# Expert stage of a decoder step: rows gathered by quarters and turned in 32x32 blocks by VectorE, gate/up weights loaded with 8 rows a partition

## The reference

```
a = jnp.einsum('td,edf->tef', t, w_gate)
b = jnp.einsum('td,edf->tef', t, w_up)
hid = (jax.nn.silu(a) * b * gates[:, :, None].astype(a.dtype)).astype(t.dtype)
out = jnp.einsum('tef,efd->td', hid, w_down)
...
x = x + g2[:, None, :] * hier_moe(h2, ...)
```

## Time and profile before

| | us |
|---|---|
| median of 3 runs | 1177.94 |
| lowest, highest | 1176.96, 1178.39 |
| span of the profiled execution (first to last instruction) | 1181.0 |
| TensorE busy | 1083.1 (92%) |
| VectorE busy | 777.0 (66%) |
| ScalarE busy | 508.2 (43%) |
| GpSimd busy | 295.5 (25%) |

### The profile page before, as it was taken

How to read it: one execution, slowest core, us unless ns; L and a number is a source line. 1 busy time by engine, 2 the same in 40 slices (tenths; PEclk the granted TensorE clock), 3 DMA queues, 4 the chain that set the end, 5 groups by cost and what they waited for, 6 DMA issues and landing times. The chain is left out here.

```text
span 1181.0 us, 18306 instructions
## 1 busy us (share of the span) xinstructions
PE 1083.1 (92%) x5541; PEld 804.7 (68%) x5542; DVE 777.0 (66%) x1276; ACT 508.2 (43%) x715; POOL 295.5 (25%) x359
## 2 busy tenths in 40 slices
PE   4799999999958899999999989999999999999992
PEld 2357777676646667777787646787878777778760
DVE  5456575756879973369887778555666555555385
ACT  5133242421132325436665344555555444444373
POOL 0046262616041000030000002333333323333344
PEclk9799999999989999999999989999999999999996
DMA  9834646557677459485766456897789777775597
GB/s 285 304 107 119 194 138 180 147 155 218 195 212 143 145 157 234 175 232 204 250 221 223 162 214 236 238 289 220 214 255 281 214 213 216 214 212 108 111 356 304
DMA packets 169247, 244.77 MB, mean 207 GB/s; under 512 B 66240, under 2 KB 124384, under 8 KB 167088
## 3 DMA queue, kind: packets, MB, share of 16 engines
q1 hardware_dynamic: 140833, 171.06, 45.8%
q0 software_dynamic: 16112, 54.88, 18.3%
q10 hardware_dynamic: 12246, 18.14, 4.6%
HBM read 169.36 MB, written 75.84 MB: 208 GB/s over the span
## 5 line engine op out<-in xcount | busy, mean ns | idle before, releaser
L126 PE MATMUL experts_psGU<-weights_we_hi,experts_x_hi 128*128 (+1 forms) x344 | 143.3, 417 | 2.7 <-issue 1.5
L128 PE MATMUL experts_psGU<-weights_we_lo,experts_x_hi 128*128 (+1 forms) x344 | 136.0, 395 | 0.0
L127 PE MATMUL experts_psGU<-weights_we_hi,experts_x_lo 128*128 (+1 forms) x344 | 135.9, 395 | 0.0
L126 PE MATMUL front_psM<-front_hT_hi,front_w_hi 128*128 128x512 f32 x256 | 107.0, 418 | 0.8 <-DVE front_hT_lo L1008 0.8
L128 PE MATMUL front_psM<-front_hT_lo,front_w_hi 128*128 128x512 f32 x256 | 101.5, 397 | 0.0
L127 PE MATMUL front_psM<-front_hT_hi,front_w_lo 128*128 128x512 f32 x256 | 101.5, 396 | 0.0
L2496 POOL DMA_INDIRECT acc_d<-experts_o_sb,experts_to_col x40 | 68.4, 1711 | 130.8 <-issue 64.8
L126 PEld LDWEIGHTS experts_psGU<-weights_we_hi,experts_x_hi 128*128 128x128 f32 x344 | 64.6, 188 | 28.5 <-issue 15.5
L2670 DVE TENSOR_TENSOR experts_x_lo<-experts_psX,experts_x_hi 128x1024 fp32r<-128x1024 f32 x42 | 51.4, 1225 | 37.5 <-ACT experts_x_hi L2560 37.5
L2660 DVE TENSOR_TENSOR weights_we_lo<-weights_we_raw,weights_we_hi (+1 forms) x64 | 75.5, 1221 | 0.0
L128 PEld LDWEIGHTS experts_psGU<-weights_we_lo,experts_x_hi 128*128 128x128 f32 x344 | 64.6, 188 | 15.5
(11 more groups left out here) (521 smaller groups left out, 2534.0 us busy)
## 6 DMA issues: line engine op xcount, KB each, us to landing
front_raw<-in_w_ada SPq DMA_DIRECT2D x32, 512.0 KB, 4.1
weights_we_raw<-in_exp_w_gate SPq DMA_DIRECT2D x16, 1024.0 KB, 6.0
weights_we_raw<-in_exp_w_up SPq DMA_DIRECT2D x16, 1024.0 KB, 12.5
weights_wd_raw<-in_exp_w_down SPq DMA_DIRECT2D x16, 1024.0 KB, 13.2
front_xraw<-in_x_prompt SPq DMA_DIRECT2D x4, 2048.0 KB, 10.7
front_raw<-in_w_ada SPq DMA_DIRECT2D x8, 1024.0 KB, 14.3
part_d<-middle_ev ACTq DMA_DIRECT2D x16, 512.0 KB, 3.0
middle_xt<-in_x_prompt SPq DMA_DIRECT2D x16, 512.0 KB, 4.7
```

Of the source, the lines that this page charges most:

```text
L126: pe.matmul(out, l_hi, r_hi, start=start, stop=False)
L127: pe.matmul(out, l_lo, r_hi, start=False, stop=False)
L128: return pe.matmul(out, l_hi, r_lo, start=False, stop=stop)
```

## The change

Three things change, and what follows from them:

1. The gate/up weights are read with 8 rows a partition, `(p k) f` instead of `(k p) f`, so that a partition's share of a matrix is one run of 8 KB in DRAM instead of 8 runs of 1 KB. `we_raw` holds gate and up apart. Index k of the contraction now stands for rows 8p + k, so the gathered rows must be turned to the same order.
2. A tile is gathered by four indirect DMAs instead of one, each with 128 pieces of 1 KB, a quarter of a row. Piece c brings, for tokens 32c to 32c+31, quarter q to the 32 partitions of quadrant q. The table of quarter indices `R.quart` is made once in `routing`: four small matmuls with `pick`, and a few steps on VectorE.
3. VectorE turns the tile with one transpose in 32x32 blocks from `xg` to `x_t`, which lies over `x_lo`. TensorE keeps only the turns of tiles 0 and 1. `x_hi` is cast from `x_t`, and `x_lo` is `x_t - x_hi` in place, both inputs in SBUF. The turn is now made two tiles ahead (`turn(s + 2)`) where it was one. The splits move: the down half and `PART1` now stand ahead of silu on ScalarE and ahead of hid on VectorE (`before`), `PART2` stays at the end (`behind`). The down half of an expert is split one tile later than before, and so its buffer is loaded later.

```
     def gather(self, pool, R, h2_d, t, u):
-        pool.tensor_copy(self.ic[:, u, :], R.idx[:, bass.ds(t, 1)]).then_inc(self.ic_ok, 1)
+        quarters = h2_d.rearrange("t (q n) -> (t q) n", q=4)
+        pool.tensor_copy(self.ic[:, u, :], R.quart[:, bass.ds(4 * t, 4)]).then_inc(self.ic_ok, 1)
         pool.wait_ge(self.ic_ok, t + 1)
         pool.sem_inc(self.fence, 1)
-        pool.indirect_dma_start(self.xg[:, u, :], None, h2_d, bass.IndirectOffsetOnAxis(self.ic[:, u, :], 0)
-                                ).then_inc(self.xg_in[u], 16)
+        for c in range(4):
+            pool.indirect_dma_start(self.xg[:, u, c * D // 4:(c + 1) * D // 4], None, quarters,
+                                    bass.IndirectOffsetOnAxis(self.ic[:, u, c:c + 1], 0)).then_inc(self.xg_in[u], 16)
...
-            sp.dma_start(self.wraw[:, u, :, i * FH:(i + 1) * FH], a[n][0, e].rearrange("(k p) f -> p k f", p=P)
-                         ).then_inc(self.raw_in[u], 16)
+            sp.dma_start(self.wraw[:, u, i], a[n][0, e].rearrange("(p k) f -> p k f", p=P)).then_inc(self.raw_in[u], 16)
...
+            def turn(t, u):
+
+                dve.wait_ge(xg_in[u], 32 * t + 16 - 32 * u)
+                dve.wait_ge(gu_mm, t - 1)
+                dve.transpose(xt[:, u].rearrange("p k (c i) -> p c k i", c=4),
+                              xg[:, u, :].rearrange("p (c j k) -> p c k j", c=4, k=KD)).then_inc(xt_ok, 1)
...
             with dve.Fori(1, end + 1, 2) as t:
                 for d in range(2):
                     u = 1 - d
                     s = t + d
-                    code = code_of(dve, s)
                     hidden_lo(s - 1)
+                    before(s)
                     hidden(s, u)
-                    x_lo_of(s + 1, 1 - u)
+                    turn(s + 2, u)
                     out(s - 1, 1 - u)
-                    with dve.If((code & 1) > 0):
-                        after = dve.snap((code >> 2) + 1)
-                        split_gu(after, PART2)
-                        split_d(after)
-                    with dve.If((code & 2) > 0):
-                        split_gu(dve.snap((code >> 2) + 2), PART1)
+                    x_lo_of(s + 2, u)
+                    behind(s)
...
@@ expert_pe
                     gate_up(s, u, now)
-                    turn(s + 1, 1 - u)
                     down(s - 1, before)
```

The new helpers on VectorE (ScalarE's are the same, with its casts):

```
+            def down_half(s):
+                code = code_of(dve, s - 1)
+                with dve.If((code & 1) > 0):
+                    split_d(dve.snap((code >> 2) + 1))
+                return code
+
+            def before(s):
+                code = down_half(s)
+                with dve.If((code & 2) > 0):
+                    split_gu(dve.snap((code >> 2) + 2), PART1)
+
+            def behind(s):
+                code = code_of(dve, s)
+                with dve.If((code & 1) > 0):
+                    split_gu(dve.snap((code >> 2) + 1), PART2)
```

154 lines of the change are left out of this document (91 added, 63 removed).

## The result

| | us |
|---|---|
| kernel before, median of 4 runs beside it | 1178.16 |
| changed kernel, median of 4 runs (lowest, highest) | 1204.71 (1203.77, 1207.84) |
| ratio | 1.0216, 95% interval 1.0199 to 1.0233 |
| predicted | 1173, range 1154 to 1192 |

The change makes the kernel 26.5 us slower. The page of the profile after has these lines: the span, busy time, TensorE's clock in 40 slices, and the shares of the chain of work that ended last.

What follows compares the result with a forecast made beforehand. The prediction took TensorE, busy 92% of the span, as the bound. Turns saved, two-tile passes, GpSimd's issues and a one-time 3 us summed as -31.2 + 11.5 + 18.0 - 3 = -4.7, from 1177.94 to 1173, range 1154 to 1192.

Steps and rivals of the forecast that it cites:

- TensorE's turns go, 31.2 us: TensorE, expert stage: 39 tile turns of 0.80 us leave the path, 31.2 us saved.
- The transpose, 2.2 us: VectorE, per tile: the new transpose of 128x1024 takes 2.2 us, bounds 1.2 to 2.3.
- GpSimd 28.6 us for three tiles: GpSimd, three-tile experts: 3 x 8.4 + 3.4 = 28.6 against TensorE's 26.6, giving back 18.0 over nine experts.
- the meetings: GpSimd issues waiting for VectorE operations with both inputs in SBUF: 3.4 us per three-tile expert, bounds nothing and 5.4.
- The first rival: GpSimd keeps up: meetings under 1.5 us per expert, only two-tile passes give back; 1158, or 1153 with cheap transpose; chance 0.27.
- With two tiles, wd_lo and the three pieces stand in one pass: VectorE, five two-tile experts: down waits, two tiles take about 20.0 instead of 17.7, giving back 11.5.
- One more read of the code table ... is inside my rounding: ScalarE and VectorE queues, per tile: a 0.32 us read, in idle time except in two-tile passes, where it is negligible.
- the three pieces of the next split come a pass later, and each is done before its user needs it ... TensorE keeps 3 x 8.87 = 26.6: VectorE splits, three-tile experts: out and hT_lo end 1 to 2 us ahead of down, so TensorE loses nothing.
- Rows too late, the slower rival, 1190: Loop of out, scatter, gather, transpose: landings lengthened beside weight loads make the kernel slower, 1190; chance 0.35.
- TensorE waiting at down ... in tiles 4, 12, 14, 16, 18: Sign that the forecast is right: TensorE waits at down or at the turn of hid in these tiles.

Runs made afterwards that it cites:

- c3: The changed kernel, four gathers kept, with unit-step transpose, splits behind x_lo and TensorE's table read once a pass: 1203.0, ratio 1.0198.
- b2: The kernel before, with each tile's rows gathered by four quarter gathers instead of one, all else as before: 1189.3, ratio 1.0072.
- g1: The changed kernel with one GpSimd copy of five indices in place of two index copies: 1204.4, ratio 1.0216.
- e1: The changed kernel with one gather of whole rows a tile instead of four, output not the reference's: 1203.5, ratio 1.0223.
- e2: The changed kernel with all splits back behind x_lo and one table read at the pass head on VectorE and ScalarE: 1203.9, ratio 1.0204.
- e4: The changed kernel with the transpose reading its columns at unit step, output not the reference's: 1208.3, ratio 1.0258.
- e9: The changed kernel with TensorE's three expert table reads a pass made as one: 1219.3, ratio 1.0316.
- g2: The changed kernel with one index copy, splits behind x_lo and TensorE's table read once, same outputs: 1182.0, ratio 1.0010.
- g4: g2 with VectorE writing the turned block into PSUM, same outputs: 1179.6, ratio 0.9994.

## Why the prediction was wrong

It said 1173, 4.7 us faster; it is 26.5 slower, a miss of 31. By its own steps:

- **TensorE's turns go, 31.2 us: right.** A tile that never waits takes 8.7 us, and without waits and slow matmuls tiles 2 to 41 take 30.1 less.
- **The transpose, 2.2 us: right** (2.18). Its two bounds were the right ones, too: 1.24 at unit step.
- **GpSimd 28.6 us for three tiles: the mechanism right, the size too small.** c3, where GpSimd alone is the limit, takes 30.7, 2.1 more, over nine such experts 19 us. 30.7 less the 25.2 that the prediction had for undisturbed issues is 5.5, where it took 3.4 for the meetings and wrote down 5.4 as the upper bound; this term was mis-sized. In c3 a gather takes 1169 ns on average against 950 undisturbed, 2.6 us over the 12 of such an expert (3.9 in the changed kernel, at 1278). The rest had no term of its own: an undisturbed cycle is 8.6 us and not 8.4, a scatter stands idle 1.52 us on average where an undisturbed one has 0.97, 1.6 us over three tiles, partly for the landing of the scatter before (25.8 us in the 390), and index copies are stretched too (the scatter's from 0.2 to 0.68 on average where it meets such an operation). One meeting, from GpSimd's and VectorE's timelines of the changed kernel:

```profile
767.75 3.00 POOL L2030 DMA_INDIRECT weights_xg<-h_d,weights_idx_col  x1 [0.80 <-POOL weights_idx_col L2026]
```

```profile
767.58 2.29 DVE L2703 TENSOR_TENSOR weights_wd_lo<-weights_wd_raw,weights_wd_hi  x1 [0.48 <-ACT weights_wd_hi L2586]
```

  The gather took 3.00 us where it takes 0.95, and ended 0.88 after wd_lo. That an issue waits for an operation with both inputs in SBUF, and not for other work of VectorE, is borne out by the counts given with b2. (The Trainium skill, SBUF — State Buffer, section "Who interferes with whom", states both that an operation with two inputs in SBUF contends with a GpSimd instruction that reads SBUF, and that tensor_tensor did not stall descriptor generation. This row and those counts agree with the first and not with the second.) The first rival, built on the second, is refuted: GpSimd doesn't keep up.
- **"With two tiles, wd_lo and the three pieces stand in one pass", about 20.0: failed, and this is the step that went wrong first.** Two tiles take 21.6. The three pieces stand with the fourth in the pass of the first tile, and wd_lo in the next. With the prediction's own prices the first of these passes is 0.42 + 3.5 + 0.48 + 2.2 + 2 x 1.23 + 1.2 = 10.3 us on VectorE, more than TensorE's tile; it measured 12.05, of which 1.78 is the wait for the first cast. "One more read of the code table ... is inside my rounding" failed with it: the read on ScalarE is 0.95 us and stands ahead of that cast.
- **"the three pieces of the next split come a pass later, and each is done before its user needs it ... TensorE keeps 3 x 8.87 = 26.6" for three tiles: failed by the same reading, and it was the second limit.** g1 and e1, where GpSimd is eased, take 30.1 and 29.8, 3.2 to 3.5 more: the first tile's down waits here too, with TensorE's own three reads and the slow matmuls behind the wait. The prediction did not have TensorE's reads at all, since before they show in three passes of 20 only, as 0.46, 0.62 and 0.46 us. (The Trainium skill, DMA: Bandwidth & Descriptors, section "Latency and other measured facts", gives some 600 ns for one tensor_load. Three would be 1.8, an estimate from that page, and the trace has 1.79; one reads as 0.53.)
- **Rows too late, the slower rival, 1190: its sign was right and its mechanism was not the change's.** In the changed kernel the transpose waits 6.9 us for rows in the 390. It waits longer (24.7 to 62.3) in e2, e4, e9 and c3, where VectorE or TensorE is eased and GpSimd's cycle is not, and 0.0 to 0.5 in e1 and g2, where the same rows are gathered with a shorter cycle. A landing time by itself was not varied.
- **"TensorE waiting at down ... in tiles 4, 12, 14, 16, 18": met by luck.** It does wait in the passes of these tiles, but for the down of the tile before, the expert's first. The sum had the down of the second tile late, one pass on, and there it never waits. It waits in three-tile experts as well, and at pass heads.
- **The clock had no term.** The 56 slow matmuls cost 10.7 us. They come behind waits, which the prediction did not have.

A further fault was in the form of the sum: it took each kind of expert to have one limit, with the rest hidden. Here two limits stood at the same height, so the loss was neither the one nor the sum.

Left open: why e9 is slower than the changed kernel (15 us, 12 by the ratios), and how the 17.0 us of the order divide between three things that moved together: the pass in which `PART1` stands, its place ahead of hid, and the code reads on ScalarE and VectorE. That `PART1` shares a pass with `PART2` is shown by the rows; what it alone costs is not, since no version had the order of the change with `PART1` in the last tile's pass.

## What to carry to other kernels

When work in a hand-written loop moves to another place in the pass, check for which tile each condition is tested, and read the order of work off the code pass by pass: here a helper returned the code of the tile before, and a split landed one tile later. When a change takes work off the engine that is the bound, list what was hidden behind it, register reads at loop heads among it, and price each as if the cover were gone. If undoing one suspect gives nothing, undo two at once before dropping either: e1 and e2 alone pointed to no cause, and together to both. Four small indirect transfers cost GpSimd four issues, and in a tight cycle a copy of an index with its wait costs as much as a transfer.

## What the runs showed of the hardware

- VectorE's transpose of 128x1024 fp32 in 32x32 blocks takes 1.24 us at unit step and 2.18 to 2.27 with a step of 8 words on the input, into SBUF (changed kernel, g2) as into PSUM (g4).
- A read of a table value into a register is hidden only as long as the engine has queued work: 0 to 0.6 us before, three in a row 1.79 after a wait, one read for three neighbouring values 0.53. On ScalarE one took 0.95.
- An index copied by GpSimd for an indirect transfer costs 0.8 to 1.0 us of wait behind a copy that itself is 0.2, or 0.77 where it begins under the issue of a scatter.
- A gather's issue that begins under a VectorE operation with both sources in SBUF waits for its end. In the changed kernel 48 began so; they took 1.92 us on average, 47 of them over 1.02, and most ended 0.81 to 0.89 after the operation. Under an x_lo with one source in PSUM (b2), 31 of 31 were not stretched (at most 1.02), nor were 66 beside a transpose.
- TensorE's granted clock was 1.00 before (2.4 GHz throughout the stage), 0.96 on average in the changed kernel and 0.99 with filler work in its waits. After some waits matmuls start 0.43 us apart instead of 0.23 (granted clock 0.51 from 876.6 to 880.0 us, the level of 1.2 GHz).
